# Even block of a four-layer network: x is turned as it lands, 1/rms goes on what its products give, x arrives on two queues and TensorE starts on a blank tile

## The chip, the cores and the metric

One core of one Trainium2 chip. The metric is the device time of one execution in microseconds (us), median of several. Five engines work side by side: TensorE (PE; its weight loads are PEld), VectorE (DVE), ScalarE (ACT), GpSimd (POOL) and SyncE (SP), which here only issues transfers. They meet at semaphores.

## What is computed

A network over 256 tokens of 1024 channels, all in float32: an even block (dilated attention beside a short gated convolution), a conv-GLU feed-forward, a retention block, a second feed-forward, then a pooling mixer, mixture-of-experts, latent attention and a second mixture-of-experts. The change lies in the first block:

```python
def rms_norm(x, g):
    xf = x.astype(jnp.float32)
    y = xf * lax.rsqrt(jnp.mean(xf * xf, axis=-1, keepdims=True) + EPS)
    return (y * g.astype(jnp.float32)).astype(x.dtype)

def even_mixer(xn, w_in, q_gain, k_gain, sconv_w, w_out):
    Bn, S, _ = xn.shape
    proj = xn @ w_in
    q, k, v, gate_b, gate_c, h = jnp.split(proj, np.cumsum(IN_SPLITS)[:-1].tolist(), axis=-1)
    heads = lambda t: t.reshape(Bn, S, A_HEADS, A_HEAD_DIM)
    q = rms_norm(heads(q), q_gain).transpose(0, 2, 1, 3)
    k = rms_norm(heads(k), k_gain).transpose(0, 2, 1, 3)
    v = heads(v).transpose(0, 2, 1, 3)
    a = dilated_attention(q, k, v).astype(xn.dtype).transpose(0, 2, 1, 3).reshape(Bn, S, A_WIDTH)
    b = gate_b * causal_dwconv(gate_c * h, sconv_w)
    return jnp.concatenate([a, b], axis=-1) @ w_out

# first block, l = 0:
x = x + even_mixer(rms_norm(x, even_norm[e]), even_w_in[e], ...)
```

Since 1/rms is one number per token, it may be multiplied onto the rows of `proj` in place of the rows of x.

## The kernel before

Tokens are two tiles (t = 0, 1) of 128 rows. A float32 product is made of three: both operands are split into a rounded high part (fp32r) and the rest, and `three_products` (L701 to L703) multiplies high by high, high by low and low by high. Weights arrive by SP's queue into a ring of units of 2 MB; the first unit comes as four quarters (L686, and L372 for the last). A unit is used in quarters: ACT rounds a quarter (`even_rounds`, L729), DVE takes the rest (`even_rests`, L736), PE multiplies. There are two buffers for quarters, so the rounding of quarter q waits until PE has used quarter q - 2 (semaphore `q_used`).

The order on each engine is that of the code; nothing reorders it.

- **Start.** SP issues the two halves of x (L2420, L2421), then the first quarters; ACT issues the constants (L2463) and the parameters (L2464). ACT squares tile 0 of x (L428, L429), DVE tile 1 (L466, L467), POOL raises to the power -1/2 (L460), DVE multiplies x by 1/rms into `hs` (L475), PE turns `hs` in 16 transposes (L520), ACT writes the high part of the turned x with the gain g put on (L443), DVE the rest (L486). Then come the first quarters on PE (`first_quarter`, L754 and L759).
- **q, k, v.** Quarters 0 to 3 give q, 4 to 7 k, 8 to 11 v (tokens on the partitions, `rows_quarter`). After q and after k ACT takes them out of PSUM: a square (L854) and a copy (L855) for each tile, with the rounding of the next quarter behind these four. DVE sums the squares by head (L913), POOL makes the heads' 1/rms (L882), DVE multiplies (L920). POOL's operation stands between k and the turning of q and k.
- **Conv inputs.** `conv_chunk` makes gate_c, h and gate_b with channels on the partitions: 12 chunks of 24 matmuls of 256 columns. The first four chunks come before the turning of q and k, the others stand between the heads.
- **Heads.** `heads_pe`, `heads_dve` and `heads_act` run eight heads, one turn i for each. In a turn DVE masks and scales the scores (L605), finds the maxima (L608, L609), takes the rest of a weight quarter (L736), divides (L617 to L620), and then runs `between(i)`: in turns 4, 6 and 8 `split_heads` (L934), in turns 2 and 4 `zT = gcT * h` (L945), in turns 2 to 5 one channel chunk of the convolution (`conv3`, L887 and two L889). PE in a turn: scores (L801, L802), one conv chunk, the transposes of the head before (L578), the values of the one before that (L590, L591).

`Chain` (called as `link(...)`) makes the engine wait for its own instruction before the next is issued.

## Time and profile before

| | |
|---|---|
| median of 3 runs | 1759.37 us (1759.12 to 1761.56) |
| the profiled execution | 1759.93 us |
| its span | 1758.1 us, 23716 instructions |
| PE busy | 1712.4 us, 97% of the span |
| PEld busy | 1136.9 us, 65% |
| DVE busy | 868.4 us, 49% |
| ACT busy | 487.3 us, 28% |
| DMA | mean 309 GB/s |

The profiled execution took 1.8 us more than its span, which is what lies around the program. Times in the rows are counted from the start of the span. An engine's busy time is no measure of where the end is set: for that, the chain of waits is followed, stretch by stretch. The even block is the first 128 us.

### The profile page before, as it was taken

Reading aid. Unit: us, or ns where it says so; the run is one execution under the profiler, and the core shown is the slowest. Engines: PE = TensorE matmul, PEld = TensorE weight load, DVE = VectorE, ACT = ScalarE, POOL = GpSimd, SP = SyncE. Lnnn points to the kernel's source line nnn. Section 1 sums busy time; section 2 is a strip of 40 time slices with the busy share of each in tenths; the row PEclk is TensorE's granted clock in tenths of the full one; section 3 lists DMA queues with packets and bytes.
Section 4 is the critical chain, followed back from the end, with each engine's and each line's share of the span. In section 5 each row is a group of like instructions: output and inputs, shape, how many; then the busy total and the mean of one; then the engine's idle time right before and its main releaser. Section 6 shows DMA issues by size and latency. Waiting matters only on the chain.

```text
span 1758.1 us, 23716 instructions
## 1 busy us (share of the span) xinstructions
PE 1712.4 (97%) x9704; PEld 1136.9 (65%) x9704; DVE 868.4 (49%) x1532; ACT 487.3 (28%) x747; POOL 22.0 (1%) x31
## 2 busy tenths in 40 slices
PE   7999999999999999999999999999999999999997
PEld 6979999987789999844444444347764444444443
DVE  5778777765658777623234233233653233232323
ACT  5555444443455444310000000013430000000001
POOL 0100000000000000000000000000000000000000
PEclk9999999999999999999999999999999999999999
DMA  9535557564545656889999999997379999999994
GB/s 372 192 120 168 188 171 236 182 196 158 184 144 168 200 167 234 319 366 418 424 426 423 429 425 425 425 419 294 146 309 405 426 424 425 424 426 426 428 423 205
DMA packets 116764, 542.42 MB, mean 309 GB/s; under 512 B 5689, under 2 KB 51905, under 8 KB 88641
## 3 DMA queue, kind: packets, MB, share of 16 engines
q1 hardware_dynamic: 116240, 539.75, 77.9%
q8 instruction: 65, 1.06, 0.2%
q10 hardware_dynamic: 432, 1.39, 0.2%
q14 instruction: 27, 0.21, 0.0%
HBM read 540.07 MB, written 1.05 MB: 308 GB/s over the span
## 4 chain that ended last, share of the span: by engine, by line
PE 87%; DMA 4%; DVE 4%; SPq 2%; ACT 1%; issue 1%; POOL 1%; DVEq 0%; ACTq 0%; POOLq 0%
PE PS L2062 23%; PE PS L2092 11%; PE PS L701 11%; PE PS L702 11%; PE PS L703 11%; PE PS L2016 6%; DMA work<-w_up 4%; PE PS L542 2%; SPq L2176 2%; PE PS L2044 2%; PE PS L2045 1%; DVE e_w_lo L736 1%; PE PS L2076 1%; PE PS L1859 1%; PE PS L1552 0%
## 5 line engine op out<-in xcount | busy, mean ns | idle before, releaser
L2062 PE MATMUL PS<-ring,work 128*64 128x512 f32 x1152 | 279.7, 593 | 0.6 <-DMA ring<-w_up 0.6
L2151 DVE SCALAR_TENSOR_TENSOR work<-PS,small,work 128x512 f32<-128x512 f32 x32 | 24.0, 751 | 405.7 <-PE PS L2062 405.7
L2062 PE MATMUL PS<-work 128*64 128x512 f32 x656 | 205.3, 595 | 0.0
L2062 PEld LDWEIGHTS PS<-ring,work 128*64 128x64 f32 x1152 | 91.4, 137 | 164.3 <-issue 164.1
L2092 PE MATMUL PS<-ring,work 128*64 128x512 f32 x576 | 160.2, 598 | 1.6 <-ACT work L2117 1.6
L2016 PEld LDWEIGHTS PS<-work,hs 128*128 128x128 f32 x1024 | 116.7, 192 | 27.5 <-issue 24.3
L2062 PEld LDWEIGHTS PS<-work 128*64 128x64 f32 x656 | 66.7, 138 | 92.0 <-issue 92.0
L2016 PE MATMUL PS<-work,hs 128*128 128x128 f32 x1024 | 122.8, 278 | 2.7 <-DVE work L1999 2.7
L2092 PE MATMUL PS<-work 128*64 128x512 f32 x368 | 124.3, 598 | 0.0
L2117 ACT ACTIVATE work<-PS 128x512 f32<-128x512 f32 x32 | 19.1, 598 | 334.8 <-PE PS L2076 334.8
L1243 DVE TENSOR_TENSOR r_w_lo<-ring,r_w_hi 128x1024 fp32r<-128x1024 f32 x64 | 78.1, 1224 | 63.6 <-ACT r_w_hi L1236 62.4
L2135 DVE TENSOR_TENSOR x_res<-x_res,PS 128x512 f32<-128x512 f32 x128 | 81.8, 681 | 50.5 <-PE PS L2045 50.4
L2113 ACT ACTIVATE work<-PS 128x512 f32<-128x512 f32 x32 | 19.1, 597 | 293.7 <-PE PS L2062 293.7
L1236 ACT ACTIVATE r_w_hi<-ring 128x1024 fp32r<-128x1024 f32 x64 | 67.9, 1065 | 113.7 <-PE PS L703 108.4
L703 PE MATMUL PS<-f_x_hi,f_w_value_lo 128*128 128x256 f32 x352 | 98.8, 281 | 0.0
L701 PE MATMUL PS<-f_x_hi,f_w_value_hi 128*128 128x256 f32 x352 | 98.8, 281 | 0.0
L702 PE MATMUL PS<-f_x_lo,f_w_value_hi 128*128 128x256 f32 x352 | 98.8, 281 | 0.0
L2092 PEld LDWEIGHTS PS<-ring,work 128*64 128x64 f32 x576 | 46.9, 136 | 75.5 <-issue 75.5
L701 PE MATMUL PS<-f_x_hi,f_w_gate_hi 128*128 128x256 f32 x320 | 90.0, 281 | 1.3 <-DVE work L1176 1.3
L702 PE MATMUL PS<-f_x_lo,f_w_gate_hi 128*128 128x256 f32 x320 | 89.8, 281 | 0.0
L703 PE MATMUL PS<-f_x_hi,f_w_gate_lo 128*128 128x256 f32 x320 | 89.8, 281 | 0.0
L2108 ACT ACTIVATE y_hi<-PS 128x512 fp32r<-128x512 f32 x62 | 37.0, 597 | 151.9 <-PE PS L2045 126.9
(370 smaller groups left out, 3438.6 us busy)
## 6 DMA issues: line engine op xcount, KB each, us to landing
ring<-w_gate SPq DMA_DIRECT2D x32, 2048.0 KB, 26.7
ring<-w_down SPq DMA_DIRECT2D x32, 2048.0 KB, 24.9
ring<-w_up SPq DMA_DIRECT2D x28, 2048.0 KB, 24.0
ring<-ffn_w_up SPq DMA_DIRECT2D x22, 2048.0 KB, 8.7
work<-w_gate SPq DMA_DIRECT2D x16, 2048.0 KB, 28.5
work<-w_down SPq DMA_DIRECT2D x14, 2048.0 KB, 21.0
work<-w_up SPq DMA_DIRECT2D x14, 2048.0 KB, 21.3
ring<-ffn_w_down SPq DMA_DIRECT2D x22, 1024.0 KB, 6.0
```

The lines of the kernel that those rows point to most:

```text
L542: last = nc.tensor.matmul(dst, lhs(c), w(c), start=(c == 0), stop=(c == n - 1))
L701: nc.tensor.matmul(dst, lhs[0], rhs[0], start=start, stop=False, skip_group_check=True)
L702: nc.tensor.matmul(dst, lhs[0], rhs[1], start=False, stop=False, skip_group_check=True)
L703: return nc.tensor.matmul(dst, lhs[1], rhs[0], start=False, stop=stop, skip_group_check=True)
L1236: nc.scalar.activation(r_w[q % 3][0][:, :], raw_quarter(units, q), ACT.Copy).then_inc(E("q_round"), 1)
L1243: nc.vector.tensor_tensor(r_w[q % 3][1][:, :], raw_quarter(units, q), r_w[q % 3][0][:, :].bitcast(F32), ALU.subtract).then_inc(E("q_split" ...
L2016: last = nc.tensor.matmul(bank(GATHER[b])[:, c * P:(c + 1) * P], hs[:, t, (4 * b + c) * P:(4 * b + c + 1) * P], sel[:, t, :], start=(t == ...
L2044: nc.tensor.matmul(bank(COMBINE[n][t]), wT[:, token], hi[:, :], start=True, stop=False)
L2062: last = nc.tensor.matmul(PS[CAP * e:CAP * (e + 1), what, :], xg[:, c, CAP * e:CAP * (e + 1)], chunk_of(w[e], c), start=(c == 0), stop=(c ...
L2092: last = nc.tensor.matmul(PS[CAP * e:CAP * (e + 1), 2 + n, :], e_hT[:, c, CAP * e:CAP * (e + 1)], part_of(w[e], c)[n], start=(c == 0), sto ...
L2108: nc.scalar.activation(hi[:, :], bank(2 + n), ACT.Copy).then_inc(q["y_hi"], 1)
L2135: nc.vector.tensor_tensor(v, v, bank(COMBINE[n][t]), ALU.add).then_inc(q["add"], 1)
```

## The change

It has these parts:

1. x is turned as it is. PE's 16 transposes read `x` and wait for its landing only; tile 0 comes first. The squares of k = 0 leave their place ahead of the norm: both tiles are squared by ACT, behind the eight copies that make the high part of the turned x. DVE's square and its two multiplications by 1/rms are gone.
2. 1/rms goes on the products. ACT's squares and copies of q, k and v take it as their scale (a value per partition). For the products with channels on the partitions, two matmuls spread 1/rms along the columns in PSUM bank 2 (two of the six idle matmuls before them make room), ACT copies that to `by_token` and its square to `by_token_2`, and DVE multiplies gcT by `by_token_2` ahead of `zT`, and each chunk of the convolution's result by `by_token`. (The convolution's result holds one more product with 1/rms for gate_b.)
3. Transfers. x tile 1 is issued by ACT behind the constants, the parameters by SP behind the first weight quarter.
4. The rounding of quarter 1 on ACT, and its rest on DVE, stand between the second and third pair of the turned x's chunks.
5. PE begins with 12 matmuls on a blank tile, which DVE clears first.
6. Waits for the clearing of kT and krT are gone, and the counts of `n_hs` are shifted by two.

```diff
@@ -230,10 +230,12 @@
 
+        blank = area(0, P)
         qk_t = area(0, NT, 2 * BANK)
...
         gbT, gcT, zT = area(5120, 4, S), area(6144, 4, S), area(7168, 4, S)
+        by_token, by_token_2 = area(4096, S), area(4096 + S, S)
         mix_hi = placed("mix_hi", [P, 8, S], work_at + 4 * 8192, F32R)
@@ -423,18 +425,17 @@
                                          scale=1.0 / D).then_inc(E("n_ms"), 1)
-            if k == 0:
-                act.wait_ge(E("first_in"), 16 * (NT + 1))
-                link(nc.scalar.activation(hs[:, 0, :], x[:, 0, :], ACT.Square, accum_out=ss[:, 0, 0:1]))
-                nc.scalar.activation(ms[:, 0:1], ss[:, 0, 0:1], ACT.Copy, bias=EPS, scale=1.0 / D).then_inc(E("n_ms"), NT)
             if k == 8:
                 return
-            if meanwhile:
+            if meanwhile and k:
                 meanwhile()
             if k == 0:
+                meanwhile(1)
                 act.wait_ge(E("param_in"), 16)
...
             for b in (range(4) if k == 6 or k in SPLIT else [1, 3]):
+                if k == 0 and b == 2:
+                    meanwhile(2)
                 act.wait_ge(E("n_tr"), 4 * k + b + 1)
@@ -446,39 +447,40 @@
                     last.then_inc(E("n_xa"), 1)
+            if k == 0:
+                for t in range(NT):
+                    link(nc.scalar.activation(sq[t], x[:, t, :], ACT.Square, accum_out=ss[:, t, 0:1]))
+                    nc.scalar.activation(ms[:, t:t + 1], ss[:, t, 0:1], ACT.Copy, bias=EPS, scale=1.0 / D).then_inc(E("n_ms"), 1)
 
...
 
-            return (1, 0) if k == 0 else (0, 1)
+            return range(NT)
 
...
             for i, t in enumerate(tiles(k)):
-                if k == i == 0:
-                    pool.wait_ge(E("ev_small"), 2)
-                else:
-                    pool.wait_ge(E("n_ms"), NT * k + i + 1)
+                pool.wait_ge(E("n_ms"), NT * k + i + 1)
                 nc.gpsimd.tensor_tensor(rstd[:, t:t + 1], ms[:, t:t + 1], C("minus_half")[:, 0:1],
...
         def norm_dve(dve, link, k, meanwhile=None):
-            if k == 0:
-                dve.wait_ge(E("first_in"), 16 * (NT + 1))
-                link(nc.vector.scalar_tensor_tensor(hs[:, 1, :], x[:, 1, :], 1.0 / D, x[:, 1, :], ALU.mult, ALU.mult, accum_out=ss[:, 1, 0:1]))
-                nc.vector.tensor_scalar(ms[:, 1:2], ss[:, 1, 0:1], EPS, None, ALU.add).then_inc(E("ev_small"), 1)
             if k in SHARED:
...
             for i, t in enumerate(tiles(k)):
+                if k == 0:
+                    break
                 dve.wait_ge(E("n_rstd"), NT * k + i + 1)
...
             if meanwhile:
-                meanwhile()
+                meanwhile() if k else meanwhile(1)
             g = G("g_kvin" if k == 6 else NORMS[k])
...
                 for b in range(4):
+                    if k == 0 and b == 2:
+                        meanwhile(2)
                     if SPLIT[k] is r_x and b == 0:
@@ -515,10 +517,11 @@
             for i, t in enumerate(tiles(k)):
-                pe.wait_ge(E("n_hs"), NT * k + i + 1)
+                if k:
+                    pe.wait_ge(E("n_hs"), NT * (k - 1) + i + 1)
                 for c in range(DC):
                     last = nc.tensor.transpose(bank(c // 2)[:, (c % 2) * S + t * P:(c % 2) * S + (t + 1) * P],
-                                               chunk(hs[:, t, :], k, c), ident)
+                                               chunk((hs if k else x)[:, t, :], k, c), ident)
                     if i == NT - 1 and c % 2:
@@ -684,6 +687,8 @@
                         sp.dma_start(view(units.slot(), DC, BANK)[:, 2 * k:2 * k + 2, :], src[:, 2 * k:2 * k + 2, :]).then_inc(E(f"quarter_in{k}"), 16)
+                        if k == 0:
+                            sp.dma_start(par[:, :], params).then_inc(E("param_in"), 16)
                     units.load(view(units.slot(), DC, BANK)[:, 6:, :], src[:, 6:, :])
@@ -780,7 +785,11 @@
 
-            idle(0, 6)
+            pe.wait_ge(E("n_rstd"), NT)
+            for t in range(NT):
+                last = nc.tensor.matmul(bank(2)[:, t * P:(t + 1) * P], rstd[:, t:t + 1].to_broadcast([P, P]), ident, start=True, stop=True)
+            last.then_inc(E("ev_tok_ps"), 1)
+            idle(0, 4)
             for i in range(2 * CONV_FIRST):
@@ -805,7 +814,6 @@
 
-            pe.wait_ge(E("ev_zero"), 2)
             heads_pe(pe, "ev", score, lambda h, t: v_t[:, t, h // 2 * P:(h // 2 + 1) * P],
@@ -844,20 +852,25 @@
 
-            norm_act(act, link, 0, lambda: rounds(2))
+            norm_act(act, link, 0, rounds)
             for n in range(3):
                 rounds(4 * n + 6)
+                if n == 0:
+                    act.wait_ge(E("n_rstd"), NT)
                 act.wait_ge(E("q_used"), 4 * n + 4)
...
                     if n < 2:
-                        nc.scalar.activation(sq[t][:, n * BANK:(n + 1) * BANK], bank(4 + 2 * n + t), ACT.Square)
-                    nc.scalar.activation(dst, bank(4 + 2 * (n % 2) + t), ACT.Copy).then_inc(E("ev_qkv"), 1)
+                        nc.scalar.activation(sq[t][:, n * BANK:(n + 1) * BANK], bank(4 + 2 * n + t), ACT.Square, scale=rstd[:, t:t + 1])
+                    nc.scalar.activation(dst, bank(4 + 2 * (n % 2) + t), ACT.Copy, scale=rstd[:, t:t + 1]).then_inc(E("ev_qkv"), 1)
+            act.wait_ge(E("ev_tok_ps"), 1)
+            nc.scalar.activation(by_token, bank(2, S), ACT.Copy).then_inc(E("ev_tok"), 1)
+            nc.scalar.activation(by_token_2, bank(2, S), ACT.Square).then_inc(E("ev_tok"), 1)
             for b in range(2):
...
                 nc.scalar.activation(gcT[:, 2 * b:2 * b + 2, :], bank(b, 2, S), ACT.Copy).then_inc(E("ev_gc"), 1)
-            act.wait_ge(E("ev_small"), 3)
+            act.wait_ge(E("ev_small"), 2)
             act.wait_ge(E("ev_qkT_ps"), 1)
@@ -878,7 +891,7 @@
         def even_pool(pool):
-            pool.wait_ge(E("ev_small"), 4)
+            pool.wait_ge(E("ev_small"), 3)
             nc.gpsimd.tensor_tensor(hrstd, hms, view(C("minus_half"), NT, 2 * A_HEADS), ALU.pow).then_inc(E("hd_rstd"), 1)
@@ -898,15 +911,11 @@
 
-            def meanwhile():
-                dve.wait_ge(E("param_in"), 16)
-                nc.vector.tensor_tensor(gqk, G("q_gain"), G("k_gain"), ALU.mult).then_inc(E("ev_small"), 1)
-                rests(2)
-
             for i in range(2):
                 other = slice((1 - i) * A_DIM, (2 - i) * A_DIM)
-                nc.vector.memset(kT[other, i, :, :], 0.0).then_inc(E("ev_zero"), 1)
-            norm_dve(dve, link, 0, meanwhile)
+                nc.vector.memset(kT[other, i, :, :], 0.0)
+            norm_dve(dve, link, 0, rests)
+            nc.vector.tensor_tensor(gqk, G("q_gain"), G("k_gain"), ALU.mult).then_inc(E("ev_small"), 1)
             rests(10)
@@ -941,14 +950,18 @@
                     dve.wait_ge(E("ev_gc"), b + 1)
+                    link(nc.vector.tensor_tensor(gcT[:, 2 * b:2 * b + 2, :], gcT[:, 2 * b:2 * b + 2, :],
+                                                 by_token_2.unsqueeze(1).to_broadcast([P, 2, S]), ALU.mult))
                     dve.wait_ge(E("q_used"), Q_CONV + 4 + 2 * (b + 1))
...
                     conv3(link, convt, zT, G("sconv"), [i - 2])
+                    link(nc.vector.tensor_tensor(convt[:, i - 2, :], convt[:, i - 2, :], by_token, ALU.mult))
 
             dve.wait_ge(E("table_in"), 16)
+            dve.wait_ge(E("ev_tok"), 2)
             heads_dve(dve, link, "ev", C("dil_mask"), A_DIM ** -0.5, between,
@@ -2418,7 +2430,6 @@
             sp.dma_start(x[:, 0, :], x_in[0, 0:P, :]).then_inc(E("first_in"), 16)
-            sp.dma_start(x[:, 1, :], x_in[0, P:S, :]).then_inc(E("first_in"), 16)
             even_load(sp, units)
@@ -2440,6 +2451,9 @@
             units = Units(pe)
+            pe.wait_ge(E("ev_small"), 1)
+            for _ in range(12):
+                nc.tensor.matmul(bank(7, P), blank, blank, start=True, stop=True)
             pe.wait_ge(E("first_in"), 16 * (NT + 1))
@@ -2461,7 +2475,7 @@
             act.dma_start(cst[:, 0:N_FIRST], const[:, 0:N_FIRST]).then_inc(E("first_in"), 16)
-            act.dma_start(par[:, :], params).then_inc(E("param_in"), 16)
+            act.dma_start(x[:, 1, :], x_in[0, P:S, :]).then_inc(E("first_in"), 16)
             link = Chain(act, E("act_link"))
@@ -2505,6 +2519,7 @@
             units = Units(dve)
+            nc.vector.memset(blank, 0.0)
             nc.vector.memset(small[:, 428:429], 0.0).then_inc(E("ev_small"), 1)
```

The order changes at two places. The first is ACT at the start of the even block, from its first instruction that reads x (e_w_hi is the rounded weight quarter, f_x_hi the high part of the turned x). Before:

```order
L428 ACTIVATE hs,small<-x_res 128x1024
L429 ACTIVATE small<-small 128x1
L729 ACTIVATE e_w_hi<-ring 128x1024 x2
L443 ACTIVATE f_x_hi<-PS,tables 128x256 x8
L729 ACTIVATE e_w_hi<-ring 128x1024 x4
```

And in the changed kernel:

```order
L734 ACTIVATE e_w_hi<-ring 128x1024
L444 ACTIVATE f_x_hi<-PS,tables 128x256 x4
L734 ACTIVATE e_w_hi<-ring 128x1024
L444 ACTIVATE f_x_hi<-PS,tables 128x256 x4
L452 ACTIVATE work,small<-x_res 128x1024
L453 ACTIVATE small<-small 128x1
L452 ACTIVATE work,small<-x_res 128x1024
L453 ACTIVATE small<-small 128x1
L734 ACTIVATE e_w_hi<-ring 128x1024 x4
```

The square of x moved from the front to a place between the turned x and the rounding of quarter 2, and there are two of them in place of one.

The second is DVE in turn 2 of the heads (work is the area that holds scores, gcT, zT and the convolution's result). Before:

```order
L945 TENSOR_TENSOR work<-work,PS 128x512 [waits q_used,ev_gc]
L887 TENSOR_SCALAR work<-work,tables 128x256 [waits ev_z]
L889 SCALAR_TENSOR_TENSOR work<-work,tables 128x255 [waits dve_link]
L889 SCALAR_TENSOR_TENSOR work<-work,tables 128x254 [waits dve_link]
L605 SCALAR_TENSOR_TENSOR work<-PS,tables 128x384 [waits at_e,at_s_ps,dve_link]
```

And in the changed kernel:

```order
L953 TENSOR_TENSOR work<-work 128x512 [waits ev_gc]
L956 TENSOR_TENSOR work<-work,PS 128x512 [waits q_used,dve_link]
L900 TENSOR_SCALAR work<-work,tables 128x256 [waits ev_z]
L902 SCALAR_TENSOR_TENSOR work<-work,tables 128x255 [waits dve_link]
L902 SCALAR_TENSOR_TENSOR work<-work,tables 128x254 [waits dve_link]
L961 TENSOR_TENSOR work<-work 128x256 [waits dve_link]
L608 SCALAR_TENSOR_TENSOR work<-PS,tables 128x384 [waits at_e,at_s_ps,dve_link]
```

Turn 2 has gained one product of 512 columns (L953) and one of 256 (L961), ahead of the next head's scores (L608). Turn 4 gains the same two, turns 3 and 5 the one of 256.

## Rows read from the trace of the kernel before

**Rows 1.** Page, part 4: shares of the chain that ended last, by engine.

```profile
PE 87%; DMA 4%; DVE 4%; SPq 2%; ACT 1%; issue 1%; POOL 1%; DVEq 0%; ACTq 0%; POOLq 0%
```

**Rows 2.** Timeline, 0 to 20 us: start, us, engine, line, op, tiles [idle before, releaser].

```profile
7.21 1.06 ACT L428 ACTIVATE hs<-x_res 128x1024 f32<-128x1024 f32 x1 [4.02 <-DMA x_res<-x]
...
8.45 0.20 ACT L429 ACTIVATE small<-small 128x1 f32<-128x1 f32 x1
...
9.14 1.06 ACT L729 ACTIVATE e_w_hi<-ring 128x1024 fp32r<-128x1024 f32 x1 [0.49 <-DMA ring<-even_w_in]
...
10.18 3.65 PE L520 MATMUL PS<-tables,hs 128*128 128x128 f32 x16 [10.18 <-DVE hs L475]
...
10.50 1.06 ACT L729 ACTIVATE e_w_hi<-ring 128x1024 fp32r<-128x1024 f32 x1 [0.30 <-DMA ring<-even_w_in]
...
12.65 3.03 ACT L443 ACTIVATE f_x_hi<-PS,tables 128x256 fp32r<-128x256 f32 x8 [1.09 <-PE PS L520]
...
13.48 0.77 PE L754 MATMUL PS<-e_w_hi,f_x_hi 128*128 128x512 f32 x1
...
16.94 1.06 ACT L729 ACTIVATE e_w_hi<-ring 128x1024 fp32r<-128x1024 f32 x1 [1.26 <-PE PS L759]
...
18.03 1.23 DVE L736 TENSOR_TENSOR e_w_lo<-ring,e_w_hi 128x1024 fp32r<-128x1024 f32 x1 [0.94 <-ACT e_w_hi L729]
...
19.43 0.40 PE L754 MATMUL PS<-e_w_hi,f_x_hi 128*128 128x512 f32 x1
```

**Rows 3.** DMA by issue, 0 to 60 us: the parameters; KB, us to landing.

```profile
tables<-params ACTq DMA_DIRECT2D x1, 509.5 KB, 6.2
```

**Rows 4.** Stretch 5 to 8 us: PE, PEld, DVE, ACT, POOL, granted clock, DMA share, GB/s.

```profile
5.00:8.00 3.00, 0.00 (x0) 0.00 (x0) 0.88 (x1) 0.79 (x1) 0.00 (x0) 1.00 1.01 378
```

**Rows 5.** ACT's copies out of PSUM, without and with a scale per partition: ns min/median/max.

```profile
L859 ACT ACTIVATE work<-PS x2: 578/580/581, 56.7 to 62.4; 128x512 f32<-128x512 f32 x2
...
L863 ACT ACTIVATE work<-PS,small x2: 680/684/687, 62.8 to 63.4; 128x512 f32<-128x512 f32 x2
```

**Rows 6.** Timeline, PEld after q's evacuation.

```profile
30.41 0.19 PEld L701 LDWEIGHTS PS<-e_w_hi,f_x_hi 128*128 128x128 f32 x1 [0.19 <-DVE e_w_lo L736]
```

**Rows 7.** Chain of waits, 36 to 50 us: start, us, what.

```profile
36.30 1.06 ACT e_w_hi L729
...
44.65 5.44 POOL small L882
```

**Rows 8.** Chain of waits, 74 to 102 us: its first rows on DVE, and its last.

```profile
74.83 0.57 DVE work L605
...
77.84 0.60 DVE work L945
78.47 0.36 DVE work L887
...
101.33 0.27 DVE work L620
```

**Rows 9.** Timeline of PE: the transposes of two successive turns of the heads.

```profile
81.96 0.49 PE L578 MATMUL PS<-tables,work 128*128 128x128 f32 x3
...
86.45 0.49 PE L578 MATMUL PS<-tables,work 128*128 128x128 f32 x3
```

**Rows 10.** Durations on DVE: ns min/median/max.

```profile
L945 DVE TENSOR_TENSOR work<-work,PS x2: 680/684/689, 77.8 to 88.1; 128x512 f32<-128x512 f32 x2
...
L736 DVE TENSOR_TENSOR e_w_lo<-ring,e_w_hi x32: 1215/1225/1227, 10.8 to 122.2; 128x1024 fp32r<-128x1024 f32 x32
```

**Rows 11.** PE after its two longest idle times behind the start, timeline.

```profile
1137.82 0.61 PE L2062 MATMUL PS<-xnT,work 128*64 128x512 f32 x1 [2.21 <-DMA work<-w_up]
...
1696.75 0.90 PE L2062 MATMUL PS<-xnT,work 128*64 128x512 f32 x1 [2.15 <-DMA work<-w_up]
```

**Rows 12.** Stretches behind these two: us, PE busy, granted clock, DMA share, GB/s.

```profile
1137.00:1141.00 4.00, 3.18 (x16) 1.00 1.01 430
...
1697.00:1700.00 3.00, 3.00 (x9) 0.50 1.01 431
```

7 lines of the change are left out of this document (3 added, 4 removed).

## The prediction

> **What bounds the kernel now.** I read the shares of the chain first: PE holds 87% of it [rows 1], so the time is PE's work plus the places where PE waits. The change touches the even block alone, so the question is how much earlier or later PE leaves that block; behind it everything shifts with it. I read four places, in order of time.
>
> At the start the chain is: x lands, squares, 1/rms, `hs`, transposes, the high part of x, the first product at 13.48 [rows 2]. The transfers run at full share (1.01 of the 16 engines, 378 GB/s at 5 to 8 us [rows 4]), so landing times are set by the bytes ahead. From the third quarter on, PE waits only for the weights' split: the rounding at 16.94, the rest at 18.03, the product at 19.43 [rows 2]. Behind q the split is late by a little again: PE had to wait 0.19 us [rows 6]. From k's evacuation to POOL and on to L920 the chain is on ACT, DVE and POOL, without a gap (from the rounding at 36.30 to POOL, 44.65 to 50.1 [rows 7]). In the heads the chain is on DVE from 74.83 to 101.33 [rows 8]: PE looks busy there, but DVE sets the pace.
>
> **The start.** The first product comes sooner. Ahead of x there is now no parameter transfer (510 KB, 1.4 us at 378 GB/s [rows 3, 4]); x landed at about 7.1 (ACT starts on it at 7.21 [rows 2]), and part of the first quarter now travels beside it, so I put it at about 6.0; the 16 transposes (3.65 us [rows 2]) end at 9.6. The parameters have the same bytes ahead as the first quarter had, which landed at 9.1 (its rounding waited until 9.14 [rows 2]): about 9.0. ACT needs them for the high part, PE for its first product: about 9.9 in place of 13.48.
>
> But this gain of 3.6 us does not last, since ACT's queue is longer ahead of the rounding of quarter 2. Its work from 9.1 on, each by the spacing of its rows: four high parts, 4 x 0.36 = 1.45 (eight took 3.03, the last 0.49 long); the rounding of quarter 1, 0.97, which can't start before that quarter's landing at 10.5 [rows 2] and here starts at 10.55; four more high parts, 1.45; two squares of x with their mean, 2 x 1.34 = 2.7 (the square at 7.21 is 1.06 long, the scaling behind it ends at 8.65, less an overlap of 0.1 [rows 2]). That ends at 15.7, where the rounding of quarter 2 starts, against 16.94 before. **Gain 1.2 us.** If the parameters land at 8.6, it is 1.4 (then the landing of quarter 1 bounds it); at 9.6, 0.7. From there the splits keep up, as before. The work taken off DVE (a square and two multiplications) and the 12 blank matmuls are worth nothing more: PE takes 3.0 us for a quarter (two from 13.48 to 19.43 [rows 2]), so the first two are done near 15.8, and it then waits for the third until about 18.1. A cold PE in them would be covered in large part too.
>
> On the DMA side the row shows both queues together at 378 GB/s and a share of 1.01 [rows 4], so a second queue adds no bandwidth; what helps x is that parameters go behind it. The Trainium skill says the same of it in "DMA: Bandwidth & Descriptors", section "Issuing engines are not separate DMA queues": issuing from several engines saves issue time only. By that rule x would land at the time set by its bytes, which is the estimate of 6.0; without that gain (x at 7.1) the transposes would end at 10.7, the high parts of the second pair would still be in time, and at most 0.5 us of the 1.2 would go.
>
> **The evacuation of q and k.** Eight operations of ACT get a scale per partition. Without one a 128x512 copy took 0.580 us, with one 0.684 [rows 5]: 0.10 more, 0.4 for a set of four. Behind q the rounding follows directly and PE already waited 0.19 for it [rows 6], so 0.4 is on the path. Behind k the set is a link of the chain itself [rows 7]: again 0.4. **Loss 0.8 us**; between 0.4 (the first is partly made up) and 0.9. The copies of v and the two of `by_token` (0.4 us each at most) fall into an idle time of ACT of over 2 us, and the two spreading matmuls take the place of two idle ones: nothing.
>
> **The heads.** DVE gains two products of 128x512 and four of 128x256, all from SBUF, all in turns 2 to 5. A product of 1024 columns takes 1.225, one of 512 (one operand in PSUM) 0.684 [rows 10]; the slope gives 0.41 for 256. Each is waited for by the next operation, about 0.04 more (77.84 + 0.60 to 78.47 [rows 8]). 2 x 0.72 + 4 x 0.45 = 3.2. Between 2.6 (if they overlap their neighbours: 0.60 and 0.35 each) and 3.6. Is there slack on DVE to take it? In the chain it has none from 74.83 to 101.33 [rows 8]. PE's turn (one conv chunk, scores, transposes, values) is 4.5 us (81.96 to 86.45 [rows 9]) against 4.4 to 6 for DVE's, so PE follows. I put through the turns with the longer DVE list: the scores stay ahead by 0.6 us or more each time, the conv chunk that waits for `zT` in turn 5 starts 2.4 later, and the last head's division is the full 3.2 later; PE then starts the output products from it. **Loss 3.2 us.**
>
> Waits removed (`ev_zero`, `ml_zero`): long fulfilled before, nothing. Waits added: ACT's first evacuation waits for POOL's 1/rms, which needs the two means (done at 15.7) while q is done at about 24; ACT's two copies wait for two matmuls at about 47, DVE's heads for those copies at about 51 and start near 67: all met early. What stands behind them in each queue is therefore not held. On SP's queue the parameters pass ahead of quarter 1, which still has the same bytes ahead of it (x, constants, parameters, quarter 0): nothing for it and what follows.
>
> **Sum:** -1.2 + 0.8 + 3.2 = +2.8 us on the profiled execution of 1759.93, so 1762.7. The median of the runs shown, 1759.37, lies 0.6 below that execution; against it the forecast is 1762.2, or +0.16%. I take 0.2% (3.5 us) as what a measurement of this kernel can tell from no change: the likeliest outcome is a small loss within it.
>
> **Rivals.**
> *The clock falls in the new idle time (slower).* PE would now wait from about 15.8 to 18.1 for quarter 2, 2.3 us, where before it had no such gap. The kernel has two idle times of about that length, 2.21 and 2.15 us [rows 11]. Behind the first the granted clock stayed at 1.00, behind the second it was 0.50 (1.2 in place of 2.4 GHz) through the 3 us from 1697 on [rows 12], 3.4 us in all. PE sets the pace behind that point, so 3.4 us at half rate cost up to 1.7: 1763.9. It decides if the clock falls at or after PE resumes; against it, that one of two rows shows no fall, and that part of a fall may lie in the gap. Chance 0.28. A related rule: the Trainium skill, "TensorE: Matmul & The Clock Gate", section "Part 4: PE-mode transpose", says that transposes in that mode don't raise the clock. By that rule the first quarters would run cold. Worked out from rows: the first product here took 0.77 us at 13.48 against 0.40 at 19.43 [rows 2], so at the low level quarter 0 ends some 2 us later, PE's gap shrinks below 1 us, and this rival dies while the sum stays. The trace speaks against the rule for these transposes, since the clock had risen shortly after 13.48, with nothing before but the 16 of them; that leaves this rival its chance.
>
> *DVE's additions are partly hidden.* If PE is the true pace in turns 3 and 5 (4.5 us against DVE's 4.4 and 4.6), or the last turns give back time, half of the 3.2 goes: 1760.6. Against it stands the chain, which names DVE throughout. Chance 0.13.
>
> *The early start carries through (faster).* If the squares did not hold the third quarter, the front would give its 3.6 us, and with hidden additions the kernel would end at 1757 or below. ACT's order excludes most of it. Chance 0.04.
>
> The forecast proper has 0.55; with the upper bounds of its terms (0.7, 0.9, 3.6) it reaches +3.8, so about 0.14 of it is above 0.2%.
>
> **Numbers.** Slower by over 0.2%: 0.14 and nearly all of the clock's 0.28, 0.40. Within: 0.57. Faster: 0.03. The range runs from 1760.0 (lower bounds and some slack) to 1764.9 (clock and upper bounds).
>
> **What would show it.** ACT's rounding of the third quarter near 15.7, with two squares ahead; PE idle some 2 us before its third quarter's products, which start near 18.1; the granted clock behind that; ACT's evacuations at 0.68; the POOL operation starting within 0.5 us of 44.65; DVE's last division of the heads 3 us later relative to POOL's start, with six new products of 0.69 and 0.41. Wrong if PE waits in the heads no longer than before (the sum falls by 3.2), or if the rounding starts before 14.5.

## The result and the profile after

| | before | changed |
|---|---|---|
| median | 1759.54 us (22 runs, 1754.89 to 1762.09) | 1762.67 us (22 runs, 1758.91 to 1765.66) |
| ratio | | 1.0017, 95% interval 1.0010 to 1.0024 |
| profiled execution | 1759.93 us | 1763.73 us |
| its span | 1758.1 us | 1761.8 us |

The change costs 3.1 us (medians), within the 0.2% that I took as the bound, though the interval reaches 0.24%. The forecast was 1762.2, +0.16%. One execution of the run called e6 below took 1792.61 us at a granted clock of 0.944; it is left out of its median.

The page of the changed kernel, its span, its busy times and the shares of the chain, says little by itself (PE held 87% of the chain before [rows 1]):

```profile
span 1761.8 us, 23770 instructions
...
PE 1717.9 (98%) x9728; PEld 1141.1 (65%) x9728; DVE 868.5 (49%) x1534; ACT 489.6 (28%) x752; POOL 21.8 (1%) x31
...
PE 85%; DMA 6%; DVE 4%; ACT 2%; SPq 1%; issue 1%; POOL 0%; DVEq 0%; ACTq 0%
```

So I read both kernels at three landmarks that the change has to pass: PE's first product of the third quarter of weights, POOL's operation on the heads' 1/rms, and PE's first output product behind the heads (us from the start of the span).

| | third quarter | POOL | output products | quarter to POOL | POOL to output |
|---|---|---|---|---|---|
| before | 19.43 | 44.65 | 103.45 | 25.22 | 58.80 |
| changed | 17.48 | 45.11 | 107.41 | 27.63 | 62.30 |
| difference | -1.95 | +0.46 | +3.96 | +2.41 | +3.50 |

The difference at the last landmark, 3.96 us, is close to that of the profiled executions (3.80), but it does not stay still in between. At POOL's later operations it is 3.94 us (at 524 us), 3.54 (at 712), 4.95 (at 1188) and 3.61 (at 1751). Most of the rise can't be the change's: a run below that moves only one transfer (e9) loses 1.2 us in the same stretch, from 733 to 1188. The fall comes at the end, where the kernel before had a low stretch of the clock at 1697 [rows 12] and the changed one had none. So it is the landmarks up to 107 us that show the change; the total of one execution shows it only to within a microsecond or so.

**The start**, the chain of waits of the changed kernel from 0 to 18 us (start, us, what), against [rows 2]:

```profile
1.21 5.85 DMA x_res<-x
7.06 0.04 issue
7.10 1.60 PE PS L523 x12
8.70 1.56 ACT f_x_hi L444 x4
10.26 0.95 ACT e_w_hi L734
11.21 1.46 ACT f_x_hi L444 x4
12.67 1.05 ACT work L452 x2
...
13.94 1.05 ACT work L452 x2
...
15.13 1.05 ACT e_w_hi L734
...
16.20 1.24 DVE e_w_lo L741
```

From 8.70 on it is ACT's queue alone: four high parts, a rounding, four high parts, two squares, and only then (15.13) the rounding of the third quarter. Its head is the transfer of x, which lands at 7.06.

The timeline of the changed kernel (start, us, engine, line, operation, and in brackets the idle time before it with what ended it) shows PE's side of it, then two of ACT's scaled copies and POOL's operation:

```profile
1.08 4.52 PE L2456 MATMUL PS<-work 128*128 128x128 f32 x24 [1.08 <-DVE small L2523]
...
7.10 2.02 PE L523 MATMUL PS<-tables,x_res 128*128 128x128 f32 x16 [1.50 <-DMA x_res<-x]
...
17.48 0.50 PE L759 MATMUL PS<-e_w_hi,f_x_hi 128*128 128x512 f32 x1 [1.80 <-DVE e_w_lo L741]
...
18.43 0.63 PE L759 MATMUL PS<-e_w_lo,f_x_hi 128*128 128x512 f32 x1
...
25.88 0.67 ACT L864 ACTIVATE work<-PS,small 128x512 f32<-128x512 f32 x1
26.45 0.68 ACT L865 ACTIVATE work<-PS,small 128x512 f32<-128x512 f32 x1
...
45.11 5.44 POOL L895 TENSOR_TENSOR small<-small,tables 128x32 f32<-128x32 f32 x1 [29.26 <-DVE small L924]
```

The blank tile's matmuls ran from 1.08, and the 16 transposes took 2.02 us against 3.65 [rows 2]. PE then stands still for 1.80 us before the third quarter, and some 0.6 us after it has resumed, its products take 0.63 in place of 0.39: the granted clock fell at 18.07, for 3.41 us. The windows of the changed kernel (us, busy times, then the granted clock as PEclk, share of the DMA engines, GB/s) show it, and the same again in the heads:

```profile
19.00:20.00 1.00, 1.00 (x4) 0.81 (x3) 0.00 (x0) 0.00 (x0) 0.00 (x0) 0.50 0.95 379
...
90.00:93.00 3.00, 1.24 (x10) 1.27 (x11) 2.83 (x6) 0.08 (x1) 0.00 (x0) 1.00 0.00 0
93.50:96.00 2.50, 2.50 (x14) 2.50 (x13) 2.30 (x5) 0.99 (x4) 0.00 (x0) 0.50 0.00 0
```

**The heads.** In the chain of the kernel before, the turn that began at 74.83 [rows 8] ends where the next one begins:

```profile
79.90 0.57 DVE work L605
```

Timeline of DVE in the changed kernel. Each L608 begins a turn; L953 and L961 are the new products:

```profile
75.33 0.56 DVE L608 SCALAR_TENSOR_TENSOR work<-PS,tables 128x384 f32<-128x384 f32 x1 [0.35 <-PE PS L811]
78.26 0.69 DVE L953 TENSOR_TENSOR work<-work 128x512 f32<-128x512 f32 x1
78.98 0.69 DVE L956 TENSOR_TENSOR work<-work,PS 128x512 f32<-128x512 f32 x1
81.13 0.43 DVE L961 TENSOR_TENSOR work<-work 128x256 f32<-128x256 f32 x1
81.59 0.56 DVE L608 SCALAR_TENSOR_TENSOR work<-PS,tables 128x384 f32<-128x384 f32 x1
...
98.56 0.56 DVE L608 SCALAR_TENSOR_TENSOR work<-PS,tables 128x384 f32<-128x384 f32 x1
102.54 0.56 DVE L608 SCALAR_TENSOR_TENSOR work<-PS,tables 128x384 f32<-128x384 f32 x1 [0.20 <-PE PS L811]
```

The turn from 74.83 to 79.90 now runs from 75.33 to 81.59: 1.19 us longer, with one product of 0.72 and one of 0.46 in it, spacing included. In the turn of the second `zT`, PE waits longest:

```profile
91.76 0.36 PE L706 MATMUL PS<-f_x_hi,e_w_hi 128*128 128x256 f32 x1 [2.73 <-DVE work L956]
```

### The profile page after: what moved, and what is told of

The parts are those of the page before. It is cut to its first block, busy times and chain, and to the rows that moved or that the text cites. A ratio compares the mean times of both kernels' runs of the same rounds, so it can differ in the third digit from the quotient of the medians.

```text
span 1761.8 us, 23770 instructions
## 1 busy us (share of the span) xinstructions
PE 1717.9 (98%) x9728; PEld 1141.1 (65%) x9728; DVE 868.5 (49%) x1534; ACT 489.6 (28%) x752; POOL 21.8 (1%) x31
## 4 chain that ended last, share of the span: by engine, by line
PE 85%; DMA 6%; DVE 4%; ACT 2%; SPq 1%; issue 1%; POOL 0%; DVEq 0%; ACTq 0%
PE PS L2074 22%; PE PS L706 11%; PE PS L2104 11%; PE PS L707 11%; PE PS L708 11%; PE PS L2028 6%; PE PS L545 2%; DMA ring<-w_gate 2%; DMA work<-w_up 2%; DMA ring<-w_up 2%; PE PS L2056 2%; PE PS L2057 1%; DVE e_w_lo L741 1%; SPq L2188 1%; PE PS L2088 1%
## 5 line engine op out<-in xcount | busy, mean ns | idle before, releaser
L2034 DVE TENSOR_TENSOR work<-PS,tables 128x512 f32<-128x512 f32 x64 | 44.2, 691 | 71.4 <-PE PS L2028 71.4
## 6 DMA issues: line engine op xcount, KB each, us to landing
ring<-w_down SPq DMA_DIRECT2D x32, 2048.0 KB, 25.3
```

Source lines behind the costliest of these rows:

```text
L2034: nc.vector.tensor_tensor(xg[:, 4 * b:4 * b + 4, :], bank(GATHER[b], 4, P), spread(g, 4, P), ALU.mult).then_inc(q["xg"], 1)
```

## The experiments

**Theory:** three terms: the start gives some 2 us up to the third quarter, and no more because ACT's squares stand ahead of its rounding; the evacuations with a scale take 0.8 back; the six products on DVE 3.3; and, in executions where it happens, a clock that falls at PE's stop before the third quarter takes up to 1.7 more. **Rivals:** the products are hidden and the loss is the clock's; the blank tile does nothing; the squares are hidden; the second queue is what brings x. All kernels but e9 start from the changed one. Verdicts of total time rest on the medians; the landmarks are of one profiled execution each.

| run | median (runs), before beside it | ratio (95%) | third quarter / POOL / output |
|---|---|---|---|
| e1 no token products | 1759.22 (11), 1760.30 | 0.9995 (0.9986 to 1.0004) | 17.44 / 43.50 / 102.34 |
| e2 no blank tile | 1763.63 (10), 1760.30 | 1.0019 (1.0010 to 1.0029) | 18.58 / 44.61 / 106.74 |
| e3 squares late | 1760.27 (11), 1760.30 | 1.0001 (0.9992 to 1.0010) | no stop / 41.51 / 103.64 |
| e4 x on SP | 1762.72 (11), 1760.30 | 1.0011 (1.0002 to 1.0020) | 17.66 / 45.24 / 107.37 |
| e5 filler | 1766.13 (5), 1759.00 | 1.0041 (1.0028 to 1.0054) | 18.29 / 44.32 / 106.62 |
| e6 q, k bare | 1761.91 (11), 1759.00 | 1.0018 (1.0009 to 1.0027) | 17.52 / 43.19 / 106.72 |
| e7 products in gaps | 1758.79 (11), 1759.00 | 1.0000 (0.9991 to 1.0009) | 17.47 / 43.49 / 102.41 |
| e8 three together | 1757.02 (12), 1759.00 | 0.9988 (0.9979 to 0.9997) | no stop / 41.35 / 100.25 |
| e9 parameters only | 1759.40 (11), 1759.11 | 1.0000 (0.9991 to 1.0009) | no stop / 44.03 / 102.80 |
| e10 more blanks | 1768.53 (5), 1759.11 | 1.0048 (1.0034 to 1.0062) | 18.20 / 44.20 / 106.49 |
| e11 e3 and e7 | 1756.13 (11), 1759.11 | 0.9979 (0.9969 to 0.9988) | no stop / 42.62 / 101.55 |

### e1: without the six products on DVE

```diff
-                    link(nc.vector.tensor_tensor(gcT[:, 2 * b:2 * b + 2, :], gcT[:, 2 * b:2 * b + 2, :],
-                                                 by_token_2.unsqueeze(1).to_broadcast([P, 2, S]), ALU.mult))
...
-                    link(nc.vector.tensor_tensor(convt[:, i - 2, :], convt[:, i - 2, :], by_token, ALU.mult))
```

> The changed kernel without DVE's six products with by_token_2 and by_token (so the convolution branch lacks 1/rms). Theory (DVE sets the pace of the heads, each added product is on the path): from POOL's heads operation to the first output product it takes 62.3 us in the changed kernel and 58.8 before; here 58.8 to 59.0, and the median falls by 3.3 to 3.5 against the changed kernel. Rival (half is hidden beside PE): 60.5 or more, median down by 1.7 or less.

POOL to output took 58.84, against 58.80 before and 62.30 changed; from the third quarter to POOL it took 0.84 more than before (26.06 against 25.22), which is what the evacuations can have cost at most. The ratio fell from 1.0017 to 0.9995: the products are on the path in full. The clock did not fall at the third quarter here, though PE had stood still nearly as long (1.74 against 1.80). First the timeline of PE in e1, then a window of e1 (columns as above, the granted clock before the last two):

```profile
17.44 0.50 PE L759 MATMUL PS<-e_w_hi,f_x_hi 128*128 128x512 f32 x1 [1.74 <-DVE e_w_lo L741]
```

```profile
19.00:20.00 1.00, 1.00 (x6) 0.82 (x5) 0.00 (x0) 0.00 (x0) 0.00 (x0) 1.00 0.93 373
```

So the stretch at the low clock and the products can be priced apart: from the third quarter to POOL, 27.63 in the changed kernel less 26.06 here is 1.57 us for 3.41 us at half rate. (e4, where the clock fell too, gives 27.58 and so 1.52.)

### e2: without the blank tile

```diff
-            pe.wait_ge(E("ev_small"), 1)
-            for _ in range(12):
-                nc.tensor.matmul(bank(7, P), blank, blank, start=True, stop=True)
```

> The changed kernel without the 12 blank matmuls. Theory read from the trace of the changed kernel: the blank tile raised the clock before x landed, so the 16 transposes took 2.0 us; without it they run at the lower level, ACT's first high part starts at about 9.8 instead of 8.69, the rounding of the third quarter at about 16.2 instead of 15.13, PE's third quarter at about 18.5 instead of 17.48. Rival (the prediction's view): the parameters bind, nothing moves by more than 0.2 us.

The timeline of e2 (columns as above):

```profile
7.29 3.68 PE L523 MATMUL PS<-tables,x_res 128*128 128x128 f32 x16 [7.29 <-DMA x_res<-x]
...
9.79 1.57 ACT L444 ACTIVATE f_x_hi<-PS,tables 128x256 fp32r<-128x256 f32 x4 [1.17 <-PE PS L523]
...
10.63 0.77 PE L759 MATMUL PS<-e_w_hi,f_x_hi 128*128 128x512 f32 x1
11.20 0.63 PE L759 MATMUL PS<-e_w_lo,f_x_hi 128*128 128x512 f32 x1
11.62 0.54 PE L759 MATMUL PS<-e_w_hi,f_x_hi 128*128 128x512 f32 x1
12.01 0.39 PE L759 MATMUL PS<-e_w_lo,f_x_hi 128*128 128x512 f32 x1
```

The transposes at the low clock last 1.66 us longer, ACT starts its high parts at 9.79 in place of 8.69, and every later step of ACT is 1.1 late. 0.19 of this is x, which landed at 7.29 in place of 7.10; the rest, 0.9 us, is what the blank tile is worth at the start. Its effect on ACT's queue is how: ACT, not PE, is what is held. Landmarks against e1, whose clock did not fall at the third quarter either: 1.14, then 1.11 at POOL. The medians can't resolve it (1.0019 against 1.0017). The products shrink from 0.77 to 0.39 near 12, with nothing but 16 transposes and three products before; e11 below shows the same with transposes alone.

### e3: the squares of x behind the third and fourth quarter's rounding

```diff
-            if k == 0:
-                for t in range(NT):
-                    link(nc.scalar.activation(sq[t], x[:, t, :], ACT.Square, accum_out=ss[:, t, 0:1]))
...
+            for t in range(NT):
+                rounds(3 + t)
+                link(nc.scalar.activation(sq[t], x[:, t, :], ACT.Square, accum_out=ss[:, t, 0:1]))
```

> The changed kernel with ACT's two squares of x put behind the rounding of quarter 2 and of quarter 3, so both roundings pass ahead. Theory (the squares hold the third quarter): its rounding starts at 12.7 to 12.8, PE's third quarter at 15.2 to 15.4 instead of 17.48, without an idle time before it and without a fall of the clock there; POOL's heads operation starts at 41.0 to 41.5 instead of 45.11 (2.2 from the start, 1.65 from the clock, where it would have fallen), the median falls by 2.2 to 3.9. Rival (the start is bound by landing and by the copies of x): POOL's operation moves by 0.5 or less beyond the clock's 1.65.

Timeline of ACT in e3:

```profile
13.10 1.06 ACT L730 ACTIVATE e_w_hi<-ring 128x1024 fp32r<-128x1024 f32 x1 [0.34 <-PE PS L760]
15.87 1.06 ACT L730 ACTIVATE e_w_hi<-ring 128x1024 fp32r<-128x1024 f32 x1 [0.43 <-PE PS L760]
```

The rounding starts at 13.10, as soon as its buffer is free (0.3 later than I expected), PE has no stop in the first quarters, and POOL is at 41.51: 1.99 earlier than with the squares in front (43.50 in e1), 3.14 earlier than before. The squares are what held the third quarter, and the early start does carry to POOL once they are out of the way: with the 0.84 of the evacuations it is 3.98 us that the start gives then. With the heads' products still in place it ends level with the kernel before.

### e4: both halves of x on SP's queue

```diff
             sp.dma_start(x[:, 0, :], x_in[0, 0:P, :]).then_inc(E("first_in"), 16)
+            sp.dma_start(x[:, 1, :], x_in[0, P:S, :]).then_inc(E("first_in"), 16)
...
-            act.dma_start(x[:, 1, :], x_in[0, P:S, :]).then_inc(E("first_in"), 16)
```

> The changed kernel with both halves of x on SP's queue, ahead of the first quarter. Theory (bytes ahead set the landing, a second queue gives nothing): x lands at 5.6 to 6.2 instead of 7.06, ACT's first high part is then bound by the parameters at 8.7 and starts where it did (8.6 to 8.8), no change of the median. Rival (the second queue is what brings x): x lands at 7.1 or later, the first high part later than 8.9.

Timeline of PE and ACT in e4:

```profile
6.00 2.04 PE L523 MATMUL PS<-tables,x_res 128*128 128x128 f32 x16 [0.19 <-DMA x_res<-x]
...
8.88 1.57 ACT L444 ACTIVATE f_x_hi<-PS,tables 128x256 fp32r<-128x256 f32 x4 [0.29 <-DMA tables<-params]
```

On one queue x is there at 6.00, the time that I had put it at; on two it is there at 7.1. (In the other traces with two queues the second half landed at 7.0 to 8.0, and in e9, again with one queue, ACT starts on it at 6.04.) From issue to landing, the transfers by queue (KB each, median us) in the changed kernel and in e4:

```profile
x_res<-x SPq DMA_DIRECT2D x1, 512.0 KB, 3.5
x_res<-x ACTq DMA_DIRECT2D x1, 512.0 KB, 5.8
```

```profile
x_res<-x SPq DMA_DIRECT2D x2, 512.0 KB, 4.2
```

The half on ACT's queue shares the engines with the first quarter of weights, which SP issues at the same moment and which on one queue stands behind it. The rule of the Trainium skill ("DMA: Bandwidth & Descriptors", section "Issuing engines are not separate DMA queues"), that a second issuing engine saves issue time only, fits in that nothing was gained; what these rows add is that the interleaving made the urgent half 1.1 us late. It costs nothing here: in e4 ACT's high parts wait for the parameters until 8.88, later than their start at 8.69 in the changed kernel, and the landmarks are within 0.2 us of that kernel's. Its clock fell too, at 18.51 for 3.41 us.

### e5: eight idle matmuls in PE's stop

```diff
+                if q == 2:
+                    for _ in range(8):
+                        nc.tensor.matmul(bank(7, P), ident, ident, start=True, stop=True)
```

> The changed kernel with 8 idle matmuls on PE between its second and third quarter, about as long as the idle time there. Theory (the idle time is what lets the clock fall to 1.2 GHz in some executions, and the fall delays the block by 1.65): no fall between 15 and 25 us, PE's third quarter at 17.4 to 17.6, POOL's heads operation at 43.4 to 43.7 as in the run without the token products, the median lower than the changed kernel's by 0.5 to 1.2. Rival (the fall has another cause): a fall at 18 to 19 us in spite of the work, POOL's operation at 45.1.

### e10: twenty blank matmuls in place of twelve

```diff
-            for _ in range(12):
+            for _ in range(20):
```

> The changed kernel with 20 blank matmuls in place of 12. They end about 7.4, so at the start they cost 0.3 us at most. Theory (the 3.1 us that PE lost in the filler run at 1191, with no wait shown, comes from the instructions added ahead of it and their place in memory, not from the filler's place): the trace shows PE waiting for nothing some 3 us within the 16 transposes near 1191, median 1765 to 1767. Rival (that stop belongs to the filler or to chance): no such stop, median 1762.5 to 1763.5.

These two are read together. In e5 the clock did not fall at the third quarter, and from there to POOL it took 26.03 us, as in e1. POOL itself came at 44.32, later than expected, because x landed at 8.02 in this execution. The absent fall proves nothing for the filler: without it the clock did not fall at this place in five of seven traces either. And the median is 7.1 us over before. The trace has a stop in the expert stage that the changed kernel does not have, 3.09 us in which PE waited for nothing that the profile shows ("issue"). It might have been the place of the filler, so e10 adds eight matmuls at the very start instead. PE's timeline in e5 and in e10:

```profile
1194.36 0.97 PE L1831 MATMUL PS<-tables,x_res 128*128 128x128 f32 x5 [3.09 <-issue]
```

```profile
1197.20 1.10 PE L1828 MATMUL PS<-tables,x_res 128*128 128x128 f32 x5 [3.06 <-issue]
```

The same stop at the same transposes, and a low stretch of the clock of 3.41 us behind it (at 1194.68 and 1197.38): together 4.9 us, by POOL's operations on either side (e5 is 3.45 us behind the kernel before at 1193 us and 8.40 at 1206, e10 6.34 and 11.22). It came with the eight added PE matmuls at either place, so neither run can show what the filler is worth in total time.

What makes the stop is not shown, but the traces hold a hint. Inside it lies a transfer of kind "instruction" (16 KB, DMA queue 8): in e5 from 1191.90 to 1193.02, in e10 from 1194.78 to 1195.90. Each starts 0.6 us behind the start of the stop, and PE goes on 1.3 us behind its end. In the changed kernel the transfer of this stretch starts at 1193.34, beside matmuls that run on. That fits a PE that waits for its own instructions; no run tests it.

e10 missed its expectation in two ways. The extra matmuls held the transposes until 8.04, and the third quarter came 0.72 us later than in the changed kernel, not 0.3. And its median, 1768.53, is above the 1765 to 1767 that I had given.

### e6: q and k taken out of PSUM without 1/rms

1/rms cancels in the heads' norm of q and k, if eps goes with it.

```diff
-                        nc.scalar.activation(sq[t][:, n * BANK:(n + 1) * BANK], bank(4 + 2 * n + t), ACT.Square, scale=rstd[:, t:t + 1])
-                    nc.scalar.activation(dst, bank(4 + 2 * (n % 2) + t), ACT.Copy, scale=rstd[:, t:t + 1]).then_inc(E("ev_qkv"), 1)
+                        nc.scalar.activation(sq[t][:, n * BANK:(n + 1) * BANK], bank(4 + 2 * n + t), ACT.Square)
+                        nc.scalar.activation(dst, bank(4 + 2 * n + t), ACT.Copy).then_inc(E("ev_qkv"), 1)
...
+            link(nc.vector.tensor_scalar(hms[:, 0, :], hss[:, 0, :], 1.0 / A_DIM, ms_part[:, 0:1], ALU.mult, ALU.add))
```

> The changed kernel with q and k copied and squared without 1/rms (it cancels in their norm by head; EPS is multiplied by the mean square instead, by three small DVE operations in place of one). Theory (each scale per partition costs ACT 0.1 us and the sets behind q and k are on the path): from PE's third quarter to POOL's operation 25.3 to 25.5 us with no fall of the clock, against 26.06 in the changed kernel and 25.22 before; median down by 0.6. Rival (no more than one set is on the path): 25.7 or more.

From the third quarter to POOL 25.67, between what I expected (25.3 to 25.5) and the rival's 25.7, against 26.06 in e1 and 25.22 before. The copies were back at 0.58 to 0.61 and a set of four at 1.91 us (2.28 with the scale), but the chain got a second small DVE operation (0.24 and 0.23 us for one of 0.18), so only 0.39 of the 0.84 came back. The median shows no gain (ratio 1.0018 against 1.0017). In this trace the clock fell in the heads, at 89.15 and for twice as long (6.83 us), at the end of a long wait of PE. PE's timeline in e6, then windows of e6:

```profile
89.83 0.55 PE L706 MATMUL PS<-f_x_hi,e_w_hi 128*128 128x256 f32 x1 [2.73 <-DVE work L961]
```

```profile
87.00:89.00 2.00, 0.10 (x1) 0.00 (x0) 1.92 (x6) 1.14 (x2) 0.00 (x0) 1.00 0.00 0
90.00:95.00 5.00, 5.00 (x24) 5.00 (x25) 4.64 (x12) 0.99 (x4) 0.00 (x0) 0.50 0.00 0
```

POOL to output took 63.53, 1.40 more than the 62.13 of e2, e3 and e4, which have the same heads and no fall in them.

### e7: the six products moved to where DVE waits anyway

The first product on gcT goes among DVE's rests before the heads, the second to the start of the heads; the four on the convolution's chunks become one on gbT behind the heads, under PE's first output products.

```diff
+            rests(17)
+            dve.wait_ge(E("ev_tok"), 2)
...
+            link(nc.vector.tensor_tensor(gcT[:, 0:2, :], gcT[:, 0:2, :],
+                                         by_token_2.unsqueeze(1).to_broadcast([P, 2, S]), ALU.mult))
...
+            link(nc.vector.tensor_tensor(gbT, gbT, by_token.unsqueeze(1).to_broadcast([P, 4, S]), ALU.mult))
+            rests(Q_OUT + 3)
```

> The changed kernel with the same products by token put where DVE is idle: gcT's between the weight splits ahead of the heads, and one product of gate_b with 1/rms behind the heads in place of the four of the convolution. Theory (the products cost time only where DVE sets the pace): from POOL's operation to the first output product 58.8 to 59.3 as without them (58.84), the output product loop not later for them, median down by 3 against the changed kernel. Rival (the places are not idle enough, DVE or PE is held there): 60.5 or more.

POOL to output took 58.92, 0.12 more than in the kernel before, with the whole computation done. The wait for `zT` is 0.64 again. e7 makes the same 2048 columns in three products in place of six, so it was their place that cost, not the work.

### e8: e3, e6 and e7 together

```diff
+                rounds(3 + t)
...
+                        nc.scalar.activation(dst, bank(4 + 2 * n + t), ACT.Copy).then_inc(E("ev_qkv"), 1)
...
+            link(nc.vector.tensor_tensor(gbT, gbT, by_token.unsqueeze(1).to_broadcast([P, 4, S]), ALU.mult))
```

> All three remedies: squares late, q and k bare, products in gaps. Theory: they add up: POOL's operation at 40.7 to 41.0, the first output product at 99.6 to 100.2 against 103.45 before and 107.41 in the changed kernel, median 3.3 to 4.0 below the kernel before, ratio 0.9977 to 0.9982. Rival (a new bound appears, for instance the landing of weights or DVE's queue at the start): ratio 0.999 or more.

### e11: e3 and e7 together, the scale on q and k kept

```diff
+                rounds(3 + t)
...
+            link(nc.vector.tensor_tensor(gbT, gbT, by_token.unsqueeze(1).to_broadcast([P, 4, S]), ALU.mult))
```

> Two remedies, squares late and products in gaps, without the bare q and k. Theory (bare q and k gained 0.39 in its run, the rest went to two small DVE operations on the chain): POOL's operation at 41.4 to 41.6, from it to the first output product 58.8 to 59.1, so that product at 100.2 to 100.7, median 0.4 above the run with all three, 1757 to 1758. Rival (the parts do not add): first output product at 101.5 or later.

Both are faster than the kernel before, e11 by 0.21% (0.12 to 0.31%), e8 by 0.12% (0.03 to 0.21%). Their intervals overlap, so they are not told apart, and the bare q and k have no gain of their own to show: POOL comes at 41.35 in e8 and at 41.51 in e3, which lacks them. e8 missed its ratio (0.9977 to 0.9982): the output products start 3.20 us earlier than before, but the span is only 2.3 shorter. 1.6 us went between 733 and 1188, where e9 loses 1.2 without any of this. e11's landmarks were late too: the output products came at 101.55, where the rival had 101.5 or later. In its profiled execution the clock had fallen at the very start, at 7.33, behind 1.97 us in which PE stood idle between the blank tile and x. PE's timeline in e11, then a window of e11:

```profile
7.33 3.61 PE L519 MATMUL PS<-tables,x_res 128*128 128x128 f32 x16 [1.97 <-DMA x_res<-x]
...
11.01 0.39 PE L755 MATMUL PS<-e_w_lo,f_x_hi 128*128 128x512 f32 x1
```

```profile
8.00:10.00 2.00, 2.00 (x12) 2.00 (x11) 1.23 (x1) 0.72 (x2) 0.00 (x0) 0.50 1.03 394
```

The transposes ran at the low clock, 3.61 us, and POOL came 1.11 us later than in e3, whose code is the same up to there. From POOL to output it took 58.93, as expected, so the parts do add and the start was late. That execution took 1758.75, the slowest of its eleven. It also shows that these transposes raise the clock by themselves: it was low from 7.33 to 10.75, PE did the 16 transposes in that time and nothing else up to 10.66, and the next products took 0.39.

### e9: the kernel before, with only the parameters behind the first quarter

```diff
+                        if k == 0:
+                            sp.dma_start(par[:, :], params).then_inc(E("param_in"), 16)
...
-            act.dma_start(par[:, :], params).then_inc(E("param_in"), 16)
```

> The kernel before with one part of the change alone: the parameters go on SP's queue behind the first weight quarter. Theory (bytes ahead set x's landing): x lands at 5.9 to 6.1 instead of 7.1 and the whole start moves with it, since squares, 1/rms and transposes hang on x: first product at 12.4 instead of 13.48, PE's third quarter at 18.3 instead of 19.43, POOL's heads operation at 43.5 to 43.7 instead of 44.65, median 1.0 lower. Rival (parameters or quarter 0, now later or earlier, bind): less than 0.4.

Timeline of e9, PE and ACT:

```profile
9.02 3.65 PE L520 MATMUL PS<-tables,hs 128*128 128x128 f32 x16 [9.02 <-DVE hs L475]
...
10.56 1.06 ACT L731 ACTIVATE e_w_hi<-ring 128x1024 fp32r<-128x1024 f32 x1 [1.57 <-DMA ring<-even_w_in]
11.53 3.01 ACT L443 ACTIVATE f_x_hi<-PS,tables 128x256 fp32r<-128x256 f32 x8
```

The transposes begin 1.16 us earlier (9.02 against 10.18 [rows 2]), but the rounding of the second quarter, whose landing did not move, stands ahead of x's high parts on ACT: the high parts start at 11.53 behind it. 0.62 us arrive at POOL and 0.65 at the output, not the 1.0 that I expected; in the total (ratio 1.0000) that is under the resolution. So an x that lands 1.1 us earlier is worth at most two thirds of a microsecond to the kernel before. The changed kernel has not even that: its x lands as late as before. Its 1.99 come with x at 7.06, from turning x without waiting for 1/rms, from the blank tile (0.9) and from the order of ACT's queue; how they divide between the first and the last was not tested.

## Why the prediction held, point by point

**The sum.** Without a fall of the clock the three terms measure -1.99 (19.43 to 17.44, e1), +0.84 (e1) and +3.33 (62.13 in e2, e3, e4 against 58.80): +2.2, against a forecast of -1.2 + 0.8 + 3.2 = +2.8. In the profiled execution the fallen clock adds 1.57 at the third quarter and 0.17 in the heads (62.30 against 62.13). The median moved by 3.1, so 0.9 us are left to explain. The granted clock is on record for every run: its mean is 0.9938 in the 22 runs of the changed kernel and 0.9945 in the 82 runs of the kernel before that stood beside the experiments. My estimate from these is 22.0 and 19.4 us at the low level in an execution, 2.6 us more (standard error 1.1). At 1.57 us for 3.41 that is 1.2 us, give or take 0.5, enough for the gap. So that the median came within 0.5 us of the forecast is partly luck: the start gave 0.8 us more than I had said, and the clock, which I had left out of the sum, took about as much.

**The start: right queue, two wrong steps that nearly cancel.** Forecast 15.7 for the rounding and 18.1 for the product, measured 15.13 and 17.48. "I put it at about 6.0" failed: x landed at 7.06, as late as before, and e4 shows the second queue as the reason. "The 12 blank matmuls are worth nothing more" failed as well: it looked only at PE in the first two quarters and not at ACT, which waits for the slow transposes; e2 shows 0.9 us. Fast transposes on a late x ended at 9.1, near the 9.6 that I had for slow ones on an early x; that is luck. The 0.6 us left of the error are ACT's high parts, which start at 8.69 in place of 9.1, and the squares, 2.46 in place of 2.7. That the squares hold the third quarter is shown by e3, where the rounding moved to 13.10.

**The evacuations.** 0.67 to 0.70 each, forecast 0.68; from the third quarter to POOL 0.84 against 0.8. The forecast took the difference of the durations, 0.10 each. What counts is the spacing: a set of four took 2.28 us (25.88 to 28.16) where it took 1.91 before (26.11 to 28.02), 0.37 each and 0.74 for both. The rest is PE's first product behind its stop, 0.34 to the next one in place of 0.23. e6 gave back only half since it lengthened another link.

**The heads.** 3.33 against 3.2; the products at 0.69 and 0.42 to 0.43 against 0.69 and 0.41. The chain's word that DVE sets the pace was enough, and e1 and e7 show it. POOL started 0.46 after 44.65, within the 0.5 that I had given, but by a longer way: the parts were -1.95, +0.84 and +1.57.

**The rivals.** The clock (0.28, priced at up to 1.7) did come in the profiled execution, at the place and for the length given, and cost 1.57. It was not sure: PE's stop before the third quarter was 1.6 to 1.9 us long in seven traces with it (changed, e1, e2, e4, e6, e7, e10), and the clock fell behind it in two (changed, e4), behind 1.80 and 1.92 us; not behind 1.89 and 1.90. What I had missed is that the wait for `zT` makes a second, longer stop: 2.73 us between the records of two matmuls. The sum had its delay (2.4 later) but the clock's rival did not count it. It stands in seven of the traces; the clock fell at its end or behind it in four (changed, e5, e6, e10), not in e2, e3 and e4. Hidden additions (0.13) are excluded by e1. "The early start carries through" (0.04) needed the squares out of the way, and e3 shows that condition to be the right one: 3.14 us at POOL.

**The transposes' clock.** By the rule of the Trainium skill ("TensorE: Matmul & The Clock Gate", section "Part 4: PE-mode transpose") transposes would not raise the clock. These traces don't agree: in e11 the clock fell at 7.33 and rose at 10.75 with nothing but the 16 transposes on PE up to 10.66, and in e2 it rose soon after 16 transposes and three products. A difference in kind remains possible: these transposes are of float32.

## What to carry to other kernels

When a scale is moved from an operand to the products, count the new operations by the engine that sets the pace where they are put: here six small DVE products in the heads cost 3.3 us, and the same scaling in DVE's waiting times 0.1 (e7). A faster start is worth what the longest queue behind it lets through: look at what else stands on that engine ahead of the next step (two squares on ACT kept back 2 of the 4 us that the new start gives). And a stop of PE that a change opens is a risk to its clock as well as a loss in itself. Closing it, as e3 does, gave both back; what filling it is worth these runs can't say.

## What the runs showed of the hardware, unexpected

- **A second queue can bring data later.** A half of x took 5.8 us on ACT's queue beside the weights on SP's, while two halves on SP's alone were there after a median of 4.2.
- **Eight more PE matmuls cost 4.9 us a thousand microseconds later**: a stop of 3.1 us of kind "issue", with a low stretch of the clock behind it, in e5 and e10. Against the changed kernel's ratio (1.0017) theirs (1.0041 and 1.0048) are 4 to 5.5 us higher. In e10 another 3.3 us were lost against the kernel before between 733 and 1188 us, where its clock was low for 10.2 us in place of 3.4. Total times of kernels that differ by a few instructions hold such shifts; the landmarks near the edit do not.
- **The clock does not fall behind every stop of about 2 us.** Nearly equal stops (1.90 and 1.92) fell on both sides, and in the heads e6 shows a low stretch of 6.83 us where the others have 3.41. Warming PE at the start is not safe either: in e11 the clock fell at 7.33 behind 1.97 us of idling before x came, in e3 it did not behind 1.69.
